# Two transformer blocks on one core: a new order of the work between the blocks

## The reference

```python
# end of block 1: feed-forward of width 2816, then the final norm
x = x + (jax.nn.silu(gate) * up) @ w_down
x = rms_norm(x, final_norm)
# block 2
mod = jax.nn.silu(c) @ w_ada + b_ada            # 6 * D numbers
sh1, sc1, ga1, sh2, sc2, ga2 = jnp.split(mod, 6)
h = rmsnorm(x, g_pre_mix) * (1.0 + sc1) + sh1
proj = h @ w_in                                  # qa, ka, va, qb, kb, vb, qi, ki, wi, gates
...                                              # rotation of q and k, top-k attention, stick-breaking attention
x = x + ga1 * rmsnorm(y, g_post_mix)
h = rmsnorm(x, g_pre_ffn) * (1.0 + sc2) + sh2
u = jax.nn.relu(h @ w_ff1)
x = x + ga2 * rmsnorm((u * u) @ w_ff2, g_post_ffn)
```

## Time and profile before

| | |
|---|---|
| median of 3 runs | 783.07 us (783.04 to 786.3) |
| profiled execution, its own time | 784.96 us |
| its span | 783.2 us, mean granted TensorE clock 0.987 |
| busy: TensorE, VectorE, ScalarE, GpSimd | 746.4, 547.7, 380.8, 53.4 us (95, 70, 49, 7%) |
| HBM read | 148.92 MB, 191 GB/s over the span |
| the stretch between the blocks | 338 to 381 us of the span |

### The profile page before, as it was taken

One profiled execution on the slowest core, in us unless ns is written; L12 is line 12 of the kernel. 1 busy time (PEld: TensorE's weight loads), 2 busy tenths in 40 slices (PEclk: granted clock), 3 DMA queues, 4 the chain that ended last, 5 costly groups with the idle time before them and its releaser, 6 DMA issues.

```text
span 783.2 us, 13196 instructions
## 1 busy us (share of the span) xinstructions
PE 746.4 (95%) x5358; PEld 688.0 (88%) x5358; DVE 547.7 (70%) x893; ACT 380.8 (49%) x524; POOL 53.4 (7%) x72
## 2 busy tenths in 40 slices
PE   5999998989999999988999999999998999999996
PEld 5998986779999999977999999999877999999985
DVE  6797778565477767795668977885766786555554
ACT  6424868563433344444545346565435444454442
POOL 2940000000000000030133000000000000000000
PEclk9999999999999999998999999999999999999999
DMA  8636320517778797851454456554532765445511
GB/s 323 220 121 240 128 96 14 189 62 304 298 292 294 295 356 287 313 189 66 164 175 168 162 213 224 192 179 162 205 117 108 260 224 208 169 167 208 206 62 54
DMA packets 27021, 151.09 MB, mean 193 GB/s; under 512 B 3128, under 2 KB 7836, under 8 KB 9564
## 3 DMA queue, kind: packets, MB, share of 16 engines
q1 hardware_dynamic: 22620, 124.81, 44.2%
q10 hardware_dynamic: 3456, 25.17, 8.2%
q0 software_dynamic: 896, 0.43, 0.3%
HBM read 148.92 MB, written 1.05 MB: 191 GB/s over the span
## 4 chain that ended last, share of the span: by engine, by line
PE 75%; DVE 15%; ACT 5%; issue 3%; DMA 1%; SPq 0%; ACTq 0%; DVEq 0%
PE ps L446 23%; PE ps L448 23%; PE ps L447 23%; DVE ada L1559 3%; DVE w_lo L1461 2%; ACT w_hi L1070 2%; DVE ada L1703 1%; PE ps L576 1%; PE ps L552 1%; DMA raw<-wts 1%; PE ps L944 1%; DVE rows_ga L1605 1%; PE ps L510 0%; ACT rows_ga L1155 0%; DVE modT L1708 0%
## 5 line engine op out<-in xcount | busy, mean ns | idle before, releaser
L1461 DVE TENSOR_TENSOR w_lo<-raw,w_hi 128x2048 fp32r<-128x2048 f32 x110 | 249.3, 2272 | 117.8 <-ACT w_hi L1070 117.6
L446 PE MATMUL ps<-h_hi,w_hi 128*128 128x256 f32 x1064 | 304.1, 286 | 4.8 <-DVE h_lo L1504 1.7
L447 PE MATMUL ps<-h_lo,w_hi 128*128 128x256 f32 x1064 | 300.9, 283 | 0.0
L448 PE MATMUL ps<-h_hi,w_lo 128*128 128x256 f32 x1064 | 300.9, 283 | 0.0
L1070 ACT CAST w_hi<-raw 128x2048 fp32r<-128x2048 f32 x110 | 205.7, 1886 | 47.2 <-PE ps L448 46.3
L446 PEld LDWEIGHTS ps<-h_hi,w_hi 128*128 128x128 f32 x1064 | 202.4, 190 | 9.7 <-issue 4.4
L447 PEld LDWEIGHTS ps<-h_lo,w_hi 128*128 128x128 f32 x1064 | 202.5, 190 | 1.9 <-issue 0.7
L448 PEld LDWEIGHTS ps<-h_hi,w_lo 128*128 128x128 f32 x1064 | 202.5, 190 | 0.3
L446 PE MATMUL ps<-w_hi,mix_hi 128*128 128x512 f32 x248 | 98.3, 396 | 3.5 <-DVE w_lo L1461 2.7
L447 PE MATMUL ps<-w_lo,mix_hi 128*128 128x512 f32 x248 | 97.4, 393 | 0.0
L448 PE MATMUL ps<-w_hi,mix_lo 128*128 128x512 f32 x248 | 97.2, 392 | 0.0
(11 more groups left out here) (275 smaller groups left out, 886.9 us busy)
## 6 DMA issues: line engine op xcount, KB each, us to landing
raw<-wts SPq DMA_DIRECT2D x113, 1024.0 KB, 4.8
ada<-w_ada ACTq DMA_DIRECT2D x24, 1024.0 KB, 6.3
resid<-x SPq DMA_DIRECT2D x2, 512.0 KB, 4.3
raw<-wts SPq DMA_DIRECT2D x2, 512.0 KB, 6.4
rows_ga<-rows_wide SPq DMA_DIRECT2D x1, 1024.0 KB, 7.3
out<-resid SPq DMA_DIRECT2D x4, 256.0 KB, 2.0
shared<-shared SPq DMA_DIRECT2D x2, 320.0 KB, 6.8
raw<-w_idx SPq DMA_DIRECT2D x1, 544.0 KB, 3.4
```

Source lines behind the costliest of these rows:

```text
L446: nc.tensor.matmul(o, lh, rh, start=start, stop=False)
L447: nc.tensor.matmul(o, lh, rl, start=False, stop=False)
L448: return nc.tensor.matmul(o, ll, rh, start=False, stop=stop)
L1461: V.tensor_tensor(w_lo[:, s % RING, 0:w], raw[:, n_of[name] % RAW, 0:w], w_hi[:, s % RING, 0:w].bitcast(F32), ALU.subtract).then_inc(w_rea ...
```

## The change

It changes the order of work and the place of one tile; what is computed stays the same.

- The sums of w_ada and their loads move from steps 2 to 9 to steps 1 to 8.
- va0's tile is loaded between gate1 and up1, and its two halves are made before step 0. va1's tile takes va0's former place in the stream and goes to a second buffer `extra_2`, in the memory of `ada`, which is free once the 16 tiles are summed. The ring thus has one tile less, and `idx` follows down10.
- down8, down9 and down10 are all taken by token halves; the last quarter of down10 comes after the transposes of the first token half. `keep_warm(4)` is gone.
- va1's products go to bank 2, so TensorE waits for the second half's adds (`x_new` 8).
- In the last step VectorE splits down10 after `hid_lo`; the modulation's adds come after that step.
- `split_rows` takes two k-tiles at once; the order on VectorE is `add_half(0)`, `scale_half(0)`, split of `idx`, `split_rows(0, ...)`, `add_half(1)`, `scale_half(1)`, `split_rows(1, ...)`. ScalarE does all eight activations of the first half before the squares of the second.
- The wide rows are loaded behind up0, after a wait for the last transposes of the attention; c's activation moves ahead of step 1.
- GpSimd clears `early` when va1 has been consumed (`x_tile` 2).

```diff
+        tiles += [("s", f"gate{i}")] + ([("x", "va0")] if i == 1 else []) + [("s", f"up{i}"), ("s", f"down{i - 1}")]
+    tiles += [("s", n) for n in ("gate9", "up9", "gate10", "up10", "down8")] + [("x", "va1")]
...
-        ada = sb("ada", [P, 2, TW])
+        with nc.sbuf_tensor("ada", [P, 2, TW], F32) as ada:
+            pass
+        extra_2 = sb("extra_2", [P, 2, TW], F32R)
...
                 if kind == "s" and s_idx[name] in ff1_tiles:
                     if s_idx[name] == FF1_LOOP:
+                        sp.wait_ge(x_ready, 1)
                         load_loop(FF1_LOOP, TURNS_1)
...
+                if name == "up0":
+                    sp.wait_ge(pT_ps, 2 * NQ)
                     sp.dma_start(rows_ga[:, :, :].rearrange("p a n -> p (a n)"), rows_wide.to_broadcast([P, 2 * D])).then_inc(s_wide, 16)
...
-            pool.wait_ge(ada_used, 17)
+            pool.wait_ge(x_tile, 2)
             nc.gpsimd.memset(early, 0.0).then_inc(partner_zero, 1)
...
-            for st in (9, 10):
+            for st in (8, 9, 10):
                 pe.wait_ge(w_ready, s_idx[f"down{st}"] + 1)
                 pe.wait_ge(hidlo_done, st + 1)
-                i = down_half(st, 0)
+                for n in range(2):
+                    i = down_half(st, 0, n)
             i.then_inc(acc_ps, 1)
-            for st in (9, 10):
-                down_half(st, 1).then_inc(pe_tile, 1)
-            keep_warm(4)
+            for st in (8, 9):
+                for n in range(2):
+                    i = down_half(st, 1, n)
+                i.then_inc(pe_tile, 1)
+            down_half(10, 1, 0)
...
             turn_half(0)
-            pe.wait_ge(x_ready, 1)
-            values_half(*xw, 0, 0, 0, DC)
-            pe.wait_ge(w_ready, s_idx["va1"] + 1)
-            values_half(*vw_, va1_bank, 0, 0, 4)
+            down_half(10, 1, 1).then_inc(pe_tile, 1)
+            pe.wait_ge(x_ready, 2)
+            values_half(*va0, x_bank["va0"], 0, 0, DC)
+            pe.wait_ge(x_new, 8)
+            values_half(*va1, x_bank["va1"], 0, 0, 4)
             turn_half(1)
...
-                if 2 <= st <= 9:
-                    load_ada(2 * (st - 2), i)
-                    load_ada(2 * (st - 2) + 1, i)
+                if 1 <= st <= 8:
+                    load_ada(2 * (st - 1), i)
+                    load_ada(2 * (st - 1) + 1, i)
...
+            act.wait_ge(ada_used, 17)
+            extra_hi("va1")
             ff1_step(10)
...
-                after(s0 + 1, i)
+                if st < FF1_STEPS - 1:
+                    after(s0 + 1, i)
...
+                if st == FF1_STEPS - 1:
+                    after(s0 + 1, i)
...
             add_half(0)
             scale_half(0)
+            after(s_idx["down8"])
+            for g in range(4):
+                split_rows(0, g)
             add_half(1)
-            for g in range(2):
-                split_rows(0, g)
             scale_half(1)
-            for g in range(2):
+            for g in range(4):
                 split_rows(1, g)
             after(s_idx["down9"])
             after(s_idx["down10"])
```

More of the change, by code:

```diff
@@ L54, in plan @@
     for i in range(1, FF1_STEPS - 2):
-        tiles += [("s", f"gate{i}"), ("s", f"up{i}"), ("s", f"down{i - 1}")]
-    tiles += [("s", n) for n in ("gate9", "up9", "gate10", "up10", "down8")] + [("x", "va0")]
-    tiles += [("s", n) for n in ("down9", "down10", "va1", "idx", "qi0", "qi1", "qa0", "qa1", "ka0", "ka1", "qb0", "qb1",
+        tiles += [("s", f"gate{i}")] + ([("x", "va0")] if i == 1 else []) + [("s", f"up{i}"), ("s", f"down{i - 1}")]
+    tiles += [("s", n) for n in ("gate9", "up9", "gate10", "up10", "down8")] + [("x", "va1")]
+    tiles += [("s", n) for n in ("down9", "down10", "idx", "qi0", "qi1", "qa0", "qa1", "ka0", "ka1", "qb0", "qb1",
                                  "kb0", "kb1", "vb0", "vb1")]
@@ L294, in evac_at @@
         def evac_at(name):
-            return 12 + s_idx[name] - s_idx["va1"]
-        extra_hi, extra_lo = extra[:, 0, :], extra[:, 1, :]
+            return 12 + s_idx[name] - s_idx["idx"]
+        extras = {"va0": (extra[:, 0, :], extra[:, 1, :]), "va1": (extra_2[:, 0, :], extra_2[:, 1, :])}
+        x_bank = {"va0": 0, "va1": 2}
         def tile_width(name):
@@ L755, in _, with down_half @@
                 ff1_step(st)
[L756 to L761, removed]
+            def down_half(st, m, n):
                 wh, wl = w3(s_idx[f"down{st}"] % RING, 2)
                 buf, ms = late_buf(st), slice(m * P, (m + 1) * P)
[L765 to L769, removed]
+                ns = slice(n * 512, (n + 1) * 512)
+                for kk in range(2):
+                    i = mm3(ps[:, 2 * m + n, :], hid_hi[buf][:, kk, ms], hid_lo[buf][:, kk, ms], wh[:, kk, ns], wl[:, kk, ns],
+                            False, st == 10 and kk == 1)
                 return i
-            for st in (9, 10):
+            for st in (8, 9, 10):
                 pe.wait_ge(w_ready, s_idx[f"down{st}"] + 1)
                 pe.wait_ge(hidlo_done, st + 1)
-                i = down_half(st, 0)
+                for n in range(2):
+                    i = down_half(st, 0, n)
             i.then_inc(acc_ps, 1)
-            for st in (9, 10):
-                down_half(st, 1).then_inc(pe_tile, 1)
-            keep_warm(4)
+            for st in (8, 9):
[3 more added lines that the diff above has]
+            down_half(10, 1, 0)
             def turn_half(m):
@@ L1243, in ff1_step, with extra_hi @@
                     after(s0 + 2, i)
+            def extra_hi(name):
+                landed(act, name)
+                nc.scalar.copy(extras[name][0], raw_of(name)).then_inc(x_hi, 1)
+            extra_hi("va0")
             ff1_step(0)
-            ff1_step(1)
             act.wait_ge(s_wide, 16)
             nc.scalar.activation(c_row, c_row, ACT.Silu).then_inc(c_ready, 1)
+            ff1_step(1)
             with act.Fori(0, TURNS_1) as i:
@@ L1253, in _ @@
             ff1_step(9)
-            landed(act, "va0")
-            nc.scalar.copy(extra_hi, raw_of("va0")).then_inc(x_hi, 1)
+            act.wait_ge(ada_used, 17)
+            extra_hi("va1")
             ff1_step(10)
             nc.scalar.preload_act_table_set("sqrt_and_others")
-            after(s_idx["down8"])
             sq_other = misc[:, 1024:2048]
@@ L1280, in _ @@
             root_half(0)
+            after(s_idx["down8"])
+            full_half(0, 0, DC)
             act.wait_ge(x_new, 8)
@@ L1293, in _ @@
             after(s_idx["down10"])
-            act.wait_ge(x_tile, 1)
-            nc.scalar.copy(z[:, VA, :], ps[:, 0, :]).then_inc(x_kept, 1)
+            for n, name in enumerate(("va0", "va1")):
+                act.wait_ge(x_tile, n + 1)
+                nc.scalar.copy(z[:, VA + n, :], ps[:, x_bank[name], :]).then_inc(x_kept, 1)
             relus = [0]
@@ L1326, in attn_b1 @@
                 nc.scalar.activation(eb, eb, ACT.Ln, bias=1.0).then_inc(b_ln, 1)
-            for s in range(s_idx["va1"], s_idx["vb1"] + 1):
+            for s in range(s_idx["idx"], s_idx["vb1"] + 1):
                 name = s_name[s]
@@ L1753, in _ @@
             dve.wait_ge(ada_used, 1)
+            extra_low("va0")
+            ff1_step(0)
+            dve.wait_ge(c_ready, 1)
+            ff1_step(1)
             with dve.Fori(0, TURNS_1) as i:
@@ L1766, in _ @@
             modulated("g_pre_mix", 8)
-            ff1_step(10)
-            after(s_idx["down8"])
             def add_half(m):
```

49 lines of the change are left out of this document (23 added, 26 removed).

## The result

The changed kernel takes 778.58 us (median of 6 runs, 776.97 to 778.95) against 785.47 for the kernel before in the same series (783.04 to 786.3). The ratio is 0.9916, 95% interval 0.990 to 0.9932: faster by 0.7 to 1.0%, some 6.6 us. The profiled execution took 778.56 us with a span of 776.8, 6.4 less than the span of before. Forecast were 6.3 us less, 776.8 us, and a range of 773.3 to 780.3. In absolute terms the result is 1.8 us above the forecast, because the forecast subtracted from the 783.07 of three runs, and the median of six runs of the kernel before is 2.4 us higher.

The account below looks back on a forecast made before the run. TensorE, busy 95% of the span, was taken as the bound, with its losses between the blocks. Counts of 6.5 and 5.9 us saved gave 6.3, so 783.07 - 6.3 = 776.8 us, range 773.3 to 780.3.

Parts of the forecast that it names:

- Sums, va1, split of down10: Last feed-forward step: earlier sums and reordered VectorE work cut TensorE's 2.5 us gap to a 0.3 us wait for down10's split.
- First norm chain: Tokens 0 to 127: rows ready at 352.6, TensorE's cover lasting to 353.4, so transposes start without a wait.
- Pairs of splits: VectorE's splits of the first token half, two k-tiles each: 0.76 us per pair, bounds 0.61 and 1.22.
- The new gap: TensorE waits 3.1 us for the second half's norm chain, from 360.5 to 363.6.
- Slow clock behind it: After the new gap TensorE loses 2.7 us, bounds 0 and 2.7; the way runs from down8's first matmul to idx's.
- Warming matmuls: Four matmuls computing nothing ahead of the first half's transposes: dropping them removes 1.7 us.
- account by losses: TensorE between the blocks: 12.3 us of gaps, slow clock and warming removed, 6.4 added, 5.9 saved.
- Cost of nothing: Feed-forward's front: up1, loaded later, is split between 181.9 and 185.6, needed at 185.17; cost 0, at most 0.5 us.
- What the first gap was: Near 344, TensorE's 2.5 us wait, explained by VectorE's queue: va0's subtraction, four sums and a 3.57 us copy before the splits.
- rival 3: GpSimd's late memset and products, held by VectorE's splits, run about 4 us beyond cover; saves 1.8, 781.3 us, chance 0.04.
- Rival 1: TensorE's clock holds through the 3.1 us gap; saves 2.7 more, 9.0 in all, 774.1 us; chance 0.14.
- rival 2: Second half's chain is longer, through costlier split pairs or a slipped first chain; saves 3.0 to 4.6, about 779.2; chance 0.14.

Follow-up runs that it names:

- down8_whole: The changed kernel with down8 taken for both token halves before down9 begins; ratio to the kernel before 0.9944.
- gap_filled: The changed kernel with six warming matmuls in its remaining gap, ahead of the second half's transposes; ratio to the kernel before 0.9905.
- before_memset_late: The kernel before with one wait changed, so GpSimd clears the exchange area only once va0 is consumed; ratio to the kernel before 0.9953.
- both_two_input: The kernel before with VectorE's eight-column copy written as a maximum and its addition of 1 as a two-input sum; ratio to the kernel before 0.9947.
- sums_late: The changed kernel with loads and sums of w_ada back in steps 2 to 9; ratio to the kernel before 0.9974.
- before_two_edits: The kernel before with the late memset and without its four warming matmuls; ratio to the kernel before 0.9941.
- copy_as_maximum: The kernel before with only the eight-column copy written as a two-input maximum; one run only, 41.02 us from down8's first matmul to idx, against 42.88.
- adds_between_splits: The changed kernel with VectorE's second-half adds between the second and third pair of splits, va0 and va1 interleaved on TensorE; ratio to the kernel before 0.9895.
- before_no_warming: The kernel before without its four warming matmuls after down10; ratio to the kernel before 1.0014.
- changed_again: The changed kernel, nothing edited, timed and profiled a second time; ratio to the kernel before 0.9930.

## Why the prediction held, step by step

Offsets are from down8's first matmul, so that the 1.69 us of the attention's clock drop out.

- **Sums, va1, split of down10.** Forecast: 0.3 us of wait. The split of down10 ended at 5.6 (343.10 + 2.29 - 339.78), and 0.2 were lost. Right.
- **First norm chain.** Forecast: adds at 8.7, transposes at 15.3 without a wait. Measured 348.56 and 355.10: 8.8 and 15.3. Right; down8_whole shows that the halves of down8 are this cover.
- **Pairs of splits** taken at 0.76 us each between 0.61 and 1.22: they start 0.74 apart (356.58, 357.32). Second adds at 19.7 forecast, 19.7 measured. Right.
- **The new gap.** 3.1 forecast, 2.82 measured, ended by VectorE's scaled rows. Right in place, 0.3 long.
- **Slow clock behind it: the mis-sized term.** I took 2.7 us, because the gap was nearest to the one of 3.0. Measured: 1.3, from 9.59 us between the second transposes and `idx` against 8.30 in down8_whole; gap_filled took the same 1.3 away. The way was forecast at 374.5 - 338.1 = 36.4 and measured at 35.18. That luck of 1.2 was spent by the later start of down8, 1.7, which the forecast didn't have; 0.5 came back near 600 us. Errors of either sign stand in a sum that came out at 6.4 for 6.3.
- **Warming matmuls** counted as 1.7 saved in the account by losses. As an item of it that is right: with the measured 0.2, 0.22 and 2.82 of gaps and 1.3 of slow clock the losses added are 4.5, and 12.3 - 4.5 = 7.8 stands against 7.7 measured. But removed alone the matmuls saved nothing, since the gap behind them grew by as much; the saving needs the other work that now fills their place.
- **Cost of nothing** for the front of the feed-forward: up1's load was late and ScalarE waited for it 3.06 us, to 179.47; its split began at 181.41 and ended at 183.6, and TensorE had no wait. Right, within the range of 181.9 to 185.6.
- **What the first gap was.** The prediction listed sums, subtraction and the long copy as VectorE's queue, and credited their move together. The sum was right, but its reading wasn't sharp: the 3.4 us of the held copy alone decided. Without them the sums and va0 could have stayed where they were, in the order of before (before_memset_late, both_two_input); in the new order the early sums are needed (sums_late). I used the port rule only to judge the memset at its new place (rival 3, which did not occur: the delay was nil), when it explained the old gap.
- Rival 1 (clock holds) did not occur, though the clock cost half of what the forecast gave it; rival 2 (longer pairs) neither. The work behind `idx` passed the lead on, and the feed-forward's stream held.

**What is shown and what is not.** An account at equal clock can be estimated from the profiles, with 0.095 us off for each slow matmul behind va0 in the order of before, and 1.3 us behind the last gap in the changed one:

| | way at equal clock, us |
|---|---|
| before | 40.2 |
| without the collision (before_memset_late and before_two_edits; 36.2 in both_two_input) | 36.0 |
| changed, but down8 whole | 35.7 |
| changed | 33.9 |

So the collision is worth some 4.2, with the slow clock behind the first gap in it, and the half tiles of down8 1.8. All other moves together are worth 0.3, the split size (0.3 in its own run) and the wide rows (nothing) among them. The remaining 1.4 of the 7.7 is slow clock, 2.7 in the profile of before and 1.3 in the changed one. Four of the five other profiles in the order of before lost only 1.1 to 1.3 there, so that part may be chance. In time the collision alone gave 3.7 us of the 5.5 that the changed kernel gave in the same series (ratios 0.9953 and 0.9930).

Not tried: by itself, the order that puts the first half's splits and activations ahead of the second half's adds and squares (in the changed kernel the stretch from the transposes to va0 is 2.44 us, 4.03 before, and TensorE's wait stands behind va0); and va1 back in the ring inside the changed order.

## What to carry to other kernels

An instruction of eight columns that takes twenty times its usual time is the first thing to ask about: here it stood in the row beside a GpSimd memset of nearly its length, and a changed wait, or another form of two tiny operations, gave more than half of what a large rearrangement did. One profile of each kernel was not enough to price the rest: compare stretches at equal clock, and look at where the next consumer starts (va0 here), not at the stretch's length alone. Before work is moved to close a gap, look for the one abnormal duration in the queue that made it. And where a chain for the second half decides, put its first link in front of work that only feeds the other engine: two pairs of splits fit into the waits of the chain itself.

## What the runs showed of the hardware

- A VectorE copy of eight columns that started together with a GpSimd memset of 128 x 4096 (3.52 us), and a tensor-with-scalar operation that started 0.4 us behind it, ended with the memset, after 3.57 and 3.15 us; with no memset beside them they took 0.17 each (before_memset_late and the changed kernel). Two-input operations of 8, 32 and 2048 columns beside the same memset kept 0.17, 0.19 and 2.29 us.
- TensorE's clock fell to the lower level behind gaps of 2.5 and 3.0 us (before), of 2.82 (changed, 0.55 for 3.7 us), and of 2.10 (copy_as_maximum, 0.65 from 347 to 350 us), but not behind gaps of 1.90 and 2.82 in down8_whole nor behind 1.29 in adds_between_splits. Behind gaps of 3.0 to 4.0 us ahead of va0, between 12 and 28 matmuls ran slow, and the longer gap did not have the more: 28 behind 2.99 (before), 14 behind 4.02 (before_no_warming). The same attention code ran from 90 to 100 us at 0.83 in one profile, 0.66 in another and 1.00 in a third (changed_again). The third gained 1.5 us on gap_filled there and lost 1.4 in a wait near 101; it starts down8 late all the same, as its matmuls between 8 and 18 us had fallen 1.8 us behind. What follows is moved by up to 2.4 us (down8 from 337.42 to 339.78), as much as some edits do.
